# Second attention of a two-block transformer kernel: transposes two units and value products three units behind the scores, three probability buffers, newest unit first on VectorE

## The chip, the cores and the metric

One core of a Trainium2 chip runs the whole program. The metric is the device time of one execution in microseconds. Its engines work side by side, each through its own list of instructions in order, and wait for each other through semaphores: TensorE (PE, with PEld for its weight loads), VectorE (DVE), ScalarE (ACT), GpSimd (POOL) and SyncE (SP), which issues the transfers of the weights.

## What is computed

A first transformer block on 256 tokens is followed by a second block of two layers on 256 latent and 256 context tokens, all in float32. The change lies in the second block's attention, which has eight heads of two 64-wide halves each:

```
s = einsum('bqhcd,bkhcd->bchqk', q, k) * 64 ** -0.5      # c: the two halves of a head
p = softmax(s, axis=-1)
a = p[:, 0] - lam * p[:, 1]
o = einsum('bhqk,bkhe->bqhe', a, v)                       # e: 128 wide
```

Latent queries attend to all 512 keys. In the first of the two layers the context queries attend to the 256 context keys as well.

## The kernel before

The attention stage runs once in layer 0 and once in layer 1 and has a barrier ahead of it and behind it. It is cut into **units**, one for a head and a block of 128 queries (`units2`, L682). Layer 0 has 32 units: numbers 0 to 15 with 512 keys (long units), 16 to 31 with 256 keys (short units). Layer 1 has the 16 long units only.

A unit u goes through seven steps:

1. `scores2` (L977, PE, matmuls L984): two products, one for each half, into a pair of PSUM banks. The pair alternates by unit (`scores_bank`, L678), so scores of u wait until the exponentials of u-2 have been read.
2. `rows2` (L1916, DVE, L1923): the row maxima of both halves, negated, in one reduction.
3. `exps2` (L1408, ACT, L1416): two exponentials with the row sum as a by-product, into the probability buffer `AT_P`. There are two such buffers, so exponentials of u wait for the transposes of u-2.
4. `probs2` (L1926, DVE, L1931 to L1935): reciprocal of both sums, times minus lambda for the second, one scaling (L1934), one scale-and-add (L1935). The instructions follow each other through a semaphore.
5. `turn2` (L988, PE, L996): two or four transposes of 128x128 into PSUM tile `PA[u % 2]`. They also wait until the output of u-2 has been read from the same tile.
6. `turned2` (L1937, DVE, L1944): one copy of the transposed probabilities to `AT_T[u % 2]`.
7. `values2` (L1000, PE, L1005) multiplies by the values into `PA[u % 2]`, and `out2` (L1420, ACT, L1423) copies the result out.

The order on each engine is written out by hand in three loops. Iteration u of PE (L1009) holds scores of u, the first half of the filling work, transposes of u-1, the second half of the filling work, and value products of u-2. Iteration u of ACT (L1426) holds the exponentials of u, its share of the filling work, and the output copy of u-2. Iteration u of DVE (L1947) is:

```
probs2(u - 1)
rows2(u)
turned2(u - 1)
beside(...)
```

**Filling work** (`attention_fill`, L82; `beside`, L810, L1285, L1686) is matrix work on streamed weights that needs the same stage as cover. Two kinds exist. Each of units 0 to 23 of layer 0 takes a modulation chunk ("ada"): 1 MB of weights, PE matmuls at L827 in PSUM pair 0, and two DVE adds of half a row (L1705). Each of units 4, 12, 20 and 28 of layer 0, and 2, 6, 10 and 14 of layer 1, takes a gate chunk ("ga"): PE matmuls at L833 and one copy each on DVE (L1914) and ACT (L1406). A chunk's matmuls wait until PSUM pair 0 has been emptied of the last one. SP refills a ring of four 1 MB slots whenever a chunk is done (L734).

After the stage's closing barrier PE computes the time-step projection (L1129), 64 matmuls, for which the next DVE work waits (L1963), while POOL and ACT start on the attention's normalisation.

Of the kernel before, what the change touches and what calls it, by code (L numbers as in the profile page):

```python
# [8 lines left out]
P = 128  # L9
# [3 lines left out]
TT = 512  # L13
# [13 lines left out]
ACT = mybir.ActivationFunctionType  # L27
# [54 lines left out]
def attention_fill(la):  # L82


    if la == -1:
        return [([("gates", GATE_AT.index(u))] if u in GATE_AT else [])
                + ([("ada0", u)] if u < ADA_CHUNKS else []) for u in range(A_UNITS)]
    units = 32 if la == 0 else 16
    every = units // 4
    return [([(f"ga{la}", u // every)] if u % every == every // 2 else [])  # L90
            + ([(f"ada{la + 1}", u)] if la == 0 and u < ADA_CHUNKS else []) for u in range(units)]
# [95 lines left out]
L_Q, L_K, L_V, L_TMP = 0, 4096, 8192, 16384  # L187
# [4 lines left out]
def program(nc, xT, stream, params, rows, consts, rel_bias, rev_hot, w_dt, scratch, cs_rows, out):  # L192
    ctx = ExitStack()
    with ctx:  # L194
# [5 lines left out]
        def sem(name):  # L200
            if name not in made:
                made[name] = ctx.enter_context(nc.semaphore(name))
            return made[name]
# [18 lines left out]
        def area(at, *shape):  # L222
            n = int(np.prod(shape))
            assert at + n <= ARENA, (at, n)
            v = work[:, at:at + n]
            names = "abcd"[:len(shape)]
            if len(shape) == 1:
                return v
            return v.rearrange(f"p ({' '.join(names)}) -> p {' '.join(names)}",
                               **{k: s for k, s in zip(names, shape)})  # L230
# [9 lines left out]
        def c_(name, i=0, n=None):  # L240
            at, m = CONSTS[name]
            return con[:, at + i:at + i + (m if n is None else n)]

        ident = c_("ident")
# [354 lines left out]
        LQ, LK, LV = area(L_Q, KT, TT), area(L_K, KT, TT), area(L_V, 4, D)  # L599
        MRG = area(L_MRG, KT, TT)  # L600
        GA = area(ARENA - 4096, KT, TT)
        AT_P = [area(L_TMP + 1024 * i, 2, TT) for i in range(2)]
        AT_T = [area(L_TMP + 2048 + 512 * i, 4, P) for i in range(2)]
        ADA = [RSTD[:, CHUNK * i:CHUNK * (i + 1)] for i in range(2)]
        ROT_T = [area(L_TMP + 4096 + 256 * i, T1) for i in range(2)]
# [72 lines left out]
        def scores_bank(u):  # L678
            return PS if u % 2 == 0 else PB[:, 1]


        def units2(la):  # L682
            lat = [(h, qt, 0, TT) for h in range(8) for qt in range(2)]
            own = [(h, 2 + qt, T1, T1) for h in range(8) for qt in range(2)]
            return lat + (own if la == 0 else [])
# [61 lines left out]
        def _(pe):  # L747
# [170 lines left out]
            for la in range(DEPTH_2):  # L918
# [23 lines left out]
                for j in range(4):  # L942
# [3 lines left out]
                    for t in range(4):  # L946
# [6 lines left out]
                        i = 4 * j + t  # L953
# [21 lines left out]
                us = units2(la)  # L975

                def scores2(u):  # L977
                    h, qt, k0, nk = us[u]
                    if u >= 2:
                        pe.wait_ge(sem("w_exp"), LAYER["w_exp"] * la + 2 * (u - 1))  # L980
                    S = scores_bank(u)
                    for cc in range(2):
                        rows_ = slice(HD * cc, HD * cc + HD)
                        mm = pe.matmul(S[:, cc, 0:nk], LQ[rows_, h, qt * P:(qt + 1) * P],  # L984
                                       LK[rows_, h, k0:k0 + nk], start=True, stop=True)
                    mm.then_inc(sem("w_scores"), 1)

                def turn2(u):  # L988
                    h, qt, k0, nk = us[u]
                    n = nk // P  # L990
                    pe.wait_ge(sem("w_probs"), LAYER["w_probs"] * la + u + 1)

                    if u >= 2:
                        pe.wait_ge(sem("w_out_read"), LAYER["w_out_read"] * la + u - 1)
                    for i in range(n):
                        mm = pe.transpose(PA[u % 2][:, i * P:(i + 1) * P],  # L996
                                          AT_P[u % 2][:, 0, i * P:(i + 1) * P], ident)
                    mm.then_inc(sem("w_turns"), 1)

                def values2(u):  # L1000
                    h, qt, k0, nk = us[u]
                    n = nk // P
                    pe.wait_ge(sem("w_turned"), LAYER["w_turned"] * la + u + 1)
                    for i in range(n):
                        mm = pe.matmul(PA[u % 2][:, 0:P], LV[:, k0 // P + i, h * P:(h + 1) * P],  # L1005
                                       AT_T[u % 2][:, i, :], start=(i == 0), stop=(i == n - 1))
                    mm.then_inc(sem("w_out"), 1)

                for u in range(len(us) + 2):  # L1009
                    if u < len(us):  # L1010
                        scores2(u)
                        beside(attention_fill(la)[u], T, 0)
                    if 1 <= u <= len(us):
                        turn2(u - 1)
                    if u < len(us):
                        beside(attention_fill(la)[u], T, 1)
                    if u >= 2:
                        values2(u - 2)
                held.finish(ada_second)
                bar()  # L1020
                def project_z(g, tiles):
# [212 lines left out]
        def _(act):  # L1234
# [3 lines left out]
            copy = nc.scalar.activation  # L1238
# [138 lines left out]
            for la in range(DEPTH_2):  # L1377
# [25 lines left out]
                us = units2(la)  # L1403
# [4 lines left out]
                def exps2(u):  # L1408
                    h, qt, k0, nk = us[u]
                    b = u % 2  # L1410

                    act.wait_ge(sem("w_max"), LAYER["w_max"] * la + u + 1)
                    if u >= 2:
                        act.wait_ge(sem("w_turns"), LAYER["w_turns"] * la + u - 1)
                    for cc in range(2):
                        copy(AT_P[b][:, cc, 0:nk], scores_bank(u)[:, cc, 0:nk], ACT.Exp,  # L1416
                             bias=STAT[:, 2 * b + cc:2 * b + cc + 1],
                             accum_out=STAT[:, 4 + 2 * b + cc:5 + 2 * b + cc]).then_inc(sem("w_exp"), 1)

                def out2(u):  # L1420
                    h, qt, k0, nk = us[u]
                    act.wait_ge(sem("w_out"), LAYER["w_out"] * la + u + 1)
                    copy(LQ[:, h, qt * P:(qt + 1) * P], PA[u % 2][:, 0:P], ACT.Copy)\  # L1423
                        .then_inc(sem("w_out_read"), 1)

                for u in range(len(us) + 2):  # L1426
                    held.finish(ada_second)
                    if u < len(us):
                        exps2(u)
                        beside(attention_fill(la)[u], ga_out)  # L1430
                    if u >= 2:
                        out2(u - 2)
                held.finish(ada_second)
                bar()

# [177 lines left out]
        def _(v):  # L1613
# [6 lines left out]
            def then(ins):  # L1620

                steps[0] += 1
                ins.then_inc(sem("dve_step"), 1)
                v.wait_ge(sem("dve_step"), steps[0])
# [230 lines left out]
            for la in range(DEPTH_2):  # L1855
# [55 lines left out]
                us = units2(la)  # L1911
# [14 lines left out]
                def probs2(u):  # L1926
                    h, qt, k0, nk = us[u]
                    b = u % 2
                    v.wait_ge(sem("w_exp"), LAYER["w_exp"] * la + 2 * u + 2)
                    r0, r1 = STAT[:, 8 + 2 * b:9 + 2 * b], STAT[:, 9 + 2 * b:10 + 2 * b]  # L1930
                    then(vec.reciprocal(STAT[:, 8 + 2 * b:10 + 2 * b], STAT[:, 4 + 2 * b:6 + 2 * b]))  # L1931
                    then(vec.tensor_tensor(r1, r1, NEG_LAM[:, la:la + 1], ALU.mult))
                    p0, p1 = AT_P[b][:, 0, 0:nk], AT_P[b][:, 1, 0:nk]
                    then(vec.tensor_scalar(p1, p1, r1, None, ALU.mult))  # L1934
                    vec.scalar_tensor_tensor(p0, p0, r0, p1, ALU.mult, ALU.add).then_inc(sem("w_probs"), 1)  # L1935

                def turned2(u):  # L1937
                    h, qt, k0, nk = us[u]
                    b = u % 2
                    n = nk // P  # L1940
                    v.wait_ge(sem("w_turns"), LAYER["w_turns"] * la + u + 1)
                    if u >= 2:
                        v.wait_ge(sem("w_out"), LAYER["w_out"] * la + u - 1)
                    vec.tensor_copy(AT_T[b][:, 0:n, :], PA[b][:, 0:nk].rearrange("p (a b) -> p a b", a=n))\  # L1944
                        .then_inc(sem("w_turned"), 1)

                for u in range(len(us) + 1):  # L1947
                    if u >= 1:
                        probs2(u - 1)
                    if u < len(us):  # L1950
                        rows2(u)
                    if u >= 1:
                        turned2(u - 1)
                    if u < len(us):
                        beside(attention_fill(la)[u], ga_out)
                bar()
# [514 lines left out]
```

## Time and profile before

| what | value |
|---|---|
| median of 3 executions | 3326.34 us (3325.12 to 3330.06) |
| profiled execution, its own time | 3327.07 us |
| span of the profiled execution | 3325.3 us |
| PE busy | 3120.7 us, 94% of the span |
| DVE busy | 1227.8 us, 37% |
| ACT busy | 689.4 us, 21% |
| POOL busy | 538.3 us, 16% |
| mean granted TensorE clock | 0.972 of full |
| attention stage of layer 0 | 963.3 to 1142.2 us |
| attention stage of layer 1 | 2473.7 to 2566.9 us |

The two stages take 272 us together, 8% of the span. The span is the time between the first and the last instruction; 1.8 us of the profiled execution lie around it. PEclk in a row is the clock that was granted to TensorE as a share of 2.4 GHz: 1.00 is 2.4 GHz and 0.50 is 1.2 GHz. In a timeline row, the number in square brackets is the time for which the engine had been idle, and behind the arrow stands whose instruction ended the idle time.

### The profile page before, as it was taken

What the parts mean: (1) busy time and instruction counts of PE and PEld (TensorE: products, weight loads), DVE (VectorE), ACT (ScalarE), POOL (GpSimd) and SP (SyncE); (2) the same over time, 40 slices, a digit from 0 to 9 for tenths busy, and PEclk for the clock granted to TensorE, in tenths of its full rate; (3) what the DMA queues carried; (4) which work ended last, traced back from release to release, by engine and by line L of the source; (5) the groups of instructions that cost most, each with busy time, mean ns of one, the idle gap of its engine ahead of it and who ended that gap; (6) DMA issues with size and microseconds to landing.
All of it is one profiled execution on the core that took longest, in us unless ns stands there. A gap on an engine that the chain in (4) does not pass through costs nothing. (4 is left out here: it accounts for less than half of the span.)

```text
span 3325.3 us, 36073 instructions
## 1 busy us (share of the span) xinstructions
PE 3120.7 (94%) x14066; PEld 2394.6 (72%) x14066; DVE 1227.8 (37%) x2407; ACT 689.4 (21%) x1549; POOL 538.3 (16%) x550
## 2 busy tenths in 40 slices
PE   8998799997999899999999999998998999989998
PEld 6765688885864546666758678887876666678887
DVE  1243222204136454656523343342235555541101
ACT  1112011101013314444430020010113244440100
POOL 0000100001210002121213324442210122210100
PEclk9999899998999899999989999999999999989999
DMA  6464234341226222222212212222211322224332
GB/s 228 159 228 165 101 123 153 134 153 67 78 102 228 76 90 102 89 98 93 76 51 89 76 64 89 89 89 76 89 64 51 109 101 102 102 89 146 139 141 99
DMA packets 60827, 365.62 MB, mean 110 GB/s; under 512 B 5818, under 2 KB 17146, under 8 KB 18320
## 3 DMA queue, kind: packets, MB, share of 16 engines
q1 hardware_dynamic: 48768, 334.65, 27.9%
q10 hardware_dynamic: 10944, 25.36, 2.1%
q0 software_dynamic: 976, 3.67, 0.3%
q8 instruction: 97, 1.59, 0.2%
q14 instruction: 42, 0.34, 0.0%
HBM read 362.38 MB, written 1.28 MB: 109 GB/s over the span
## 5 line engine op out<-in xcount | busy, mean ns | idle before, releaser
L348 PE MATMUL PB<-H,ring 128*128 128x256 f32 (+1 forms) x2048 | 471.5, 394 | 26.9 <-ACT H L1387 20.7
L348 PEld LDWEIGHTS PB<-H,ring 128*128 128x128 f32 x2048 | 395.5, 194 | 102.9 <-issue 45.0
L1050 PE MATMUL PB<-H,ring 128*128 128x512 f32 (+1 forms) x1024 | 430.1, 567 | 0.0
L1050 PEld LDWEIGHTS PB<-H,ring 128*128 128x128 f32 x1024 | 192.9, 191 | 181.8 <-issue 175.6
L388 PE MATMUL PB<-work,ring 128*128 128x256 f32 x1280 | 279.7, 382 | 8.2 <-POOLq L284 7.2
L388 PEld LDWEIGHTS PB<-work,ring 128*128 128x128 f32 x1280 | 244.8, 191 | 43.0 <-issue 9.3
L1997 DVE SCALAR_TENSOR_TENSOR work<-PB,par,work 128x510 f32<-128x510 f32 (+3 forms) x256 | 182.1, 713 | 14.8 <-ACT work L1458 8.0
L1031 PE MATMUL PB<-ring,H 128*128 128x256 f32 x768 | 174.5, 382 | 4.9 <-DVE work L1997 4.9
L833 PE MATMUL PB<-H,ring 128*128 128x256 f32 (+1 forms) x640 | 177.6, 432 | 0.9 <-ACT mod L1282 0.9
L492 POOL TENSOR_TENSOR sums<-ring 128x512 f32<-128x512 f32 x53 | 68.4, 1290 | 670.9 <-PE PA L459 231.4
L348 PE MATMUL PB<-work,ring 128*128 128x256 f32 (+1 forms) x544 | 155.2, 447 | 7.7 <-POOLq L284 5.0
L1031 PEld LDWEIGHTS PB<-ring,H 128*128 128x128 f32 x768 | 143.1, 190 | 23.6 <-issue 5.7
L833 PEld LDWEIGHTS PB<-H,ring 128*128 128x128 f32 x640 | 121.1, 194 | 48.6 <-issue 35.0
L1502 ACT ACTIVATE work<-sums,work 128x128 f32<-128x128 f32 x384 | 119.0, 396 | 163.5 <-PE PA L1112 163.5
L459 PE MATMUL PB<-work,sums 128*128 128x256 f32 x680 | 150.8, 379 | 0.0
L348 PEld LDWEIGHTS PB<-work,ring 128*128 128x128 f32 x544 | 104.4, 193 | 56.9 <-issue 37.2
L459 PEld LDWEIGHTS PB<-work,sums 128*128 128x128 f32 x680 | 129.2, 190 | 17.6
L2297 POOL TENSOR_TENSOR work<-work 128x256 f32<-128x256 f32 x128 | 83.8, 679 | 289.3 <-PE PA L1112 289.3
L2281 POOL TENSOR_TENSOR work<-work 128x256 f32<-128x256 f32 x96 | 62.2, 667 | 381.8 <-ACT work L1482 312.7
L1112 PEld LDWEIGHTS PA<-work 128*128 128x128 f32 x768 | 102.2, 206 | 23.6 <-issue 11.5
L459 PE MATMUL PA<-work,sums 128*128 128x256 f32 x528 | 118.5, 379 | 0.0
L1841 DVE SCALAR_TENSOR_TENSOR work<-PB,par,work 128x254 f32<-128x254 f32 (+1 forms) x128 | 55.8, 477 | 169.0 <-ACT work L1361 164.8
(315 smaller groups left out, 4251.8 us busy)
## 6 DMA issues: line engine op xcount, KB each, us to landing
ring<-stream SPq DMA_DIRECT2D x315, 1024.0 KB, 4.8
sums<-cs_rows ACTq DMA_DIRECT2D x16, 1024.0 KB, 4.7
sums<-cs_rows ACTq DMA_DIRECT2D x16, 512.0 KB, 4.0
work<-scratch POOLq DMA_DIRECT2D x1, 2560.0 KB, 13.9
X<-xT SPq DMA_DIRECT2D x2, 1024.0 KB, 15.3
out<-H SPq DMA_DIRECT2D x1, 1024.0 KB, 4.8
con<-consts SPq DMA_DIRECT2D x1, 716.0 KB, 17.8
wdt<-w_dt POOLq DMA_DIRECT2D x1, 512.0 KB, 10.4
```

The costliest lines, as they stand in the source:

```text
L348: mm = pe.matmul(PB[:, pair, t, 0:T], ring[:, c % SLOTS, k, t * P:(t + 1) * P], rhs(k), start=(k == 0), stop=(k == KT - 1))
L388: mm = pe.matmul(PB[:, pair, t, 0:T], ring[:, c % SLOTS, k, t * P:(t + 1) * P], rhs(KT * part + k), start=(part == 0 and k == 0), stop=(pa ...
L459: mm = pe.matmul(fast_bank(side, bank)[:, col:col + T1], weight(k), right(4 * part + k), start=first and opens and k == 0, stop=last and k ...
L492: nc.gpsimd.tensor_tensor(su[:, 0], a21, a22, ALU.add).then_inc(sem("w_summed"), 1)
L833: mm = pe.matmul(PB[:, pair, t, 0:T], ring[:, c % SLOTS, k, t * P:(t + 1) * P], H[:, k, 0:T], start=(k == 0), stop=(k == KT - 1))
L1031: mm = pe.matmul(PB[:, pair, t // per, col:col + CHUNK], H[:, k, t * P:(t + 1) * P], ring[:, c % SLOTS, k, :], start=(k == 0), stop=(k == ...
L1050: mm = pe.matmul(PB[:, pair, t, 0:Tc], ring[:, c % SLOTS, k, t * P:(t + 1) * P], H[:, k, 0:Tc], start=(k == 0), stop=(k == KT - 1))
L1112: mm = pe.matmul(PA[t // 2][:, 256 * (t % 2) + HD * r:256 * (t % 2) + HD * r + HD], MB[r % 2][:, d, t, :], XC[r % 2][:, d, t, :], start=(d ...
L1502: ins = copy(MB[r % 2][:, d, t, :], BC[:, hp % 2, r % 2, d, t * P:(t + 1) * P], ACT.Relu, scale=-1.0, bias=CS[:, t, hh:hh + 1])
L1997: ins = vec.scalar_tensor_tensor(dst, src, par[:, W0 + 32 * tap + ch:W0 + 32 * tap + ch + 1], dst, ALU.mult, ALU.add)
L2281: gp.tensor_tensor(XD[d].rearrange("p (a b) -> p a b", a=4), XG[:, t, :].rearrange("p (a b) -> p a b", a=4), WD[:, t, heads].unsqueeze(2). ...
L2297: gp.tensor_tensor(XC[r % 2][:, d, :, :], XG[:, :, HD * r:HD * r + HD], DT[:, :, hh:hh + 1].broadcast_to([P, 4, HD]), ALU.mult)\
```

## The change

A third probability buffer is added in free memory. On PE the transposes move from one unit behind the scores to two, and the value products from two to three. On ACT the output copy moves from two units behind to three, and exponentials of u wait for the transposes of u-3 in place of u-2. On DVE an iteration takes the row maxima of the newest unit first, then the probabilities of the unit before, then the copy of the transposes of the unit before that. No instruction other than waits is added to or taken from a unit, and each loop gains one iteration at its end. The filling work keeps its unit numbers.

```diff
-        AT_P = [area(L_TMP + 1024 * i, 2, TT) for i in range(2)]
+        AT_P = [area(L_TMP + at_, 2, TT) for at_ in (0, 1024, 4608)]
...
-                for u in range(len(us) + 2):
+                for u in range(len(us) + 3):
                     if u < len(us):
                         scores2(u)
                         beside(attention_fill(la)[u], T, 0)
-                    if 1 <= u <= len(us):
-                        turn2(u - 1)
+                    if 2 <= u <= len(us) + 1:
+                        turn2(u - 2)
                     if u < len(us):
                         beside(attention_fill(la)[u], T, 1)
-                    if u >= 2:
-                        values2(u - 2)
+                    if u >= 3:
+                        values2(u - 3)
...
-                    if u >= 2:
-                        act.wait_ge(sem("w_turns"), LAYER["w_turns"] * la + u - 1)
+                    if u >= 3:
+                        act.wait_ge(sem("w_turns"), LAYER["w_turns"] * la + u - 2)
...
-                for u in range(len(us) + 2):
+                for u in range(len(us) + 3):
                     held.finish(ada_second)
                     if u < len(us):
                         exps2(u)
                         beside(attention_fill(la)[u], ga_out)
-                    if u >= 2:
-                        out2(u - 2)
+                    if u >= 3:
+                        out2(u - 3)
...
-                for u in range(len(us) + 1):
-                    if u >= 1:
-                        probs2(u - 1)
+                for u in range(len(us) + 2):
                     if u < len(us):
                         rows2(u)
-                    if u >= 1:
-                        turned2(u - 1)
+                    if 1 <= u <= len(us):
+                        probs2(u - 1)
+                    if u >= 2:
+                        turned2(u - 2)
                     if u < len(us):
                         beside(attention_fill(la)[u], ga_out)
```

Where a step reads or writes `AT_P`, the index `u % 2` becomes `u % 3`; all other buffers keep two copies.

## Rows read from the trace of the kernel before

**Rows 1.** Busy time by engine in stretches: both attention stages, one short unit.

```profile
core 0: us, PE busy (x) PEld busy (x) DVE busy (x) ACT busy (x) POOL busy (x), PEclk, DMA share, GB/s
963.30:1142.20 178.90, 153.70 (x937) 80.21 (x937) 100.62 (x243) 51.77 (x169) 0.00 (x0) 0.97 0.48 170
2473.70:2566.90 93.20, 73.89 (x384) 53.73 (x384) 54.97 (x101) 29.40 (x85) 0.00 (x0) 0.95 0.16 56
1097.50:1100.70 3.20, 2.71 (x26) 1.44 (x26) 2.49 (x9) 1.30 (x5) 0.00 (x0) 1.00 1.00 364
```

**Rows 2.** Waits in layer 1's attention stage: who waits for whom, total, times, longest.

```profile
PE PA L996 <- DVE work L1935: 18.3, 8, 5.1
...
DVE small L1931 <- ACT work L1416: 12.8, 12, 2.9
```

**Rows 3.** Timeline, one plain unit of layer 1: start, duration, engine, line.

```profile
2499.40 1.22 DVE L1923 TENSOR_REDUCE small<-PS 128x2 f32<-128x1024 f32 x1
...
2499.54 0.66 PE L996 MATMUL PA<-con,work 128*128 128x128 f32 x4 [1.76 <-DVE work L1935]
...
2500.53 0.68 DVE L1944 COPY work<-PA 128x512 f32<-128x512 f32 x1
...
2501.02 1.13 PE L984 MATMUL PB<-work 64*128 64x512 f32 x4
...
2502.13 0.17 DVE L1931 RECIPROCAL small<-small 128x2 f32<-128x2 f32 x1 [0.92 <-ACT work L1416]
...
2503.71 1.22 DVE L1923 TENSOR_REDUCE small<-PB 128x2 f32<-128x1024 f32 x1
```

**Rows 4.** Timeline, one long unit of layer 0 with a modulation chunk.

```profile
1010.05 1.22 DVE L1923 TENSOR_REDUCE small<-PB 128x2 f32<-128x1024 f32 x1
...
1010.19 0.66 PE L996 MATMUL PA<-con,work 128*128 128x128 f32 x4 [0.51 <-DVE work L1935]
...
1012.79 0.17 DVE L1931 RECIPROCAL small<-small 128x2 f32<-128x2 f32 x1 [0.38 <-ACT work L1416]
...
1012.87 1.13 PE L984 MATMUL PS<-work 64*128 64x512 f32 x4
...
1014.37 1.22 DVE L1923 TENSOR_REDUCE small<-PS 128x2 f32<-128x1024 f32 x1
```

**Rows 5.** Timeline, short units of layer 0: with a chunk, then without.

```profile
1099.13 0.49 DVE L1705 TENSOR_TENSOR rstd<-PB,rstd 128x128 f32<-128x128 f32 x2 [0.61 <-PE PB L827]
...
1100.85 0.44 PE L996 MATMUL PA<-con,work 128*128 128x128 f32 x2 [0.51 <-DVE work L1935]
...
1108.59 0.17 DVE L1931 RECIPROCAL small<-small 128x2 f32<-128x2 f32 x1 [0.73 <-ACT work L1416]
```

**Rows 6.** Timeline, a unit of layer 1 with a gate chunk beside it.

```profile
2548.79 1.13 PE L984 MATMUL PS<-work 64*128 64x512 f32 x4
...
2551.48 1.22 DVE L1923 TENSOR_REDUCE small<-PS 128x2 f32<-128x1024 f32 x1
...
2558.28 1.13 PE L984 MATMUL PB<-work 64*128 64x512 f32 x4
...
2559.46 1.23 DVE L1923 TENSOR_REDUCE small<-PB 128x2 f32<-128x1024 f32 x1
```

**Rows 7.** Timeline, the first units of layer 0 and of layer 1.

```profile
968.75 0.17 DVE L1931 RECIPROCAL small<-small 128x2 f32<-128x2 f32 x1 [2.46 <-ACT work L1416]
...
974.65 1.22 DVE L1923 TENSOR_REDUCE small<-PS 128x2 f32<-128x1024 f32 x1
...
2479.11 0.17 DVE L1931 RECIPROCAL small<-small 128x2 f32<-128x2 f32 x1 [2.85 <-ACT work L1416]
...
2485.01 1.22 DVE L1923 TENSOR_REDUCE small<-PS 128x2 f32<-128x1024 f32 x1
```

**Rows 8.** Timeline, the last row of layer 1's attention stage.

```profile
2566.55 0.28 ACT L1423 ACTIVATE work<-PA 128x128 f32<-128x128 f32 x1 [0.77 <-PE PA L1005]
```

**Rows 9.** Stretches behind each attention stage (columns as in rows 1).

```profile
1142.20:1155.00 12.80, 12.80 (x60) 12.80 (x61) 0.00 (x0) 6.18 (x3) 2.04 (x2) 0.50 0.00 0
2566.90:2574.30 7.40, 7.38 (x65) 7.39 (x66) 0.00 (x0) 4.48 (x3) 1.18 (x2) 1.00 0.00 0
```

More of the change, by code:

```diff
@@ L996, in turn2 @@
                         mm = pe.transpose(PA[u % 2][:, i * P:(i + 1) * P],
-                                          AT_P[u % 2][:, 0, i * P:(i + 1) * P], ident)
+                                          AT_P[u % 3][:, 0, i * P:(i + 1) * P], ident)
                     mm.then_inc(sem("w_turns"), 1)
@@ L1412, in exps2 @@
                     act.wait_ge(sem("w_max"), LAYER["w_max"] * la + u + 1)
-                    if u >= 2:
-                        act.wait_ge(sem("w_turns"), LAYER["w_turns"] * la + u - 1)
+                    if u >= 3:
+                        act.wait_ge(sem("w_turns"), LAYER["w_turns"] * la + u - 2)
                     for cc in range(2):
-                        copy(AT_P[b][:, cc, 0:nk], scores_bank(u)[:, cc, 0:nk], ACT.Exp,
+                        copy(AT_P[u % 3][:, cc, 0:nk], scores_bank(u)[:, cc, 0:nk], ACT.Exp,
                              bias=STAT[:, 2 * b + cc:2 * b + cc + 1],
@@ L1932, in probs2 @@
                     then(vec.tensor_tensor(r1, r1, NEG_LAM[:, la:la + 1], ALU.mult))
-                    p0, p1 = AT_P[b][:, 0, 0:nk], AT_P[b][:, 1, 0:nk]
+                    p0, p1 = AT_P[u % 3][:, 0, 0:nk], AT_P[u % 3][:, 1, 0:nk]
                     then(vec.tensor_scalar(p1, p1, r1, None, ALU.mult))
```

## Prediction, made before the changed kernel was run

> **What bounds the kernel now.** I first read the share of busy time: PE is busy for 94% of the span, so time is lost mostly where PE waits. Then I cut out the two attention stages. In layer 1's stage of 93.2 us PE is busy for 73.9 us and DVE for 55.0, and in layer 0's stage of 178.9 us for 153.7 and 100.6 [rows 1]: neither is full, so something is waiting in a circle. The waits name it: PE waits for DVE's last probability step, and DVE's reciprocal waits for ACT's exponentials [rows 2].
>
> One plain unit of layer 1 shows the circle. DVE starts the row maxima at 2499.40, its reciprocal can only start at 2502.13, when the maxima and both exponentials have run (2.73 us), and the next maxima start 1.58 us later, behind the four probability steps [rows 3]. Maxima, exponentials, probabilities, next maxima: 2.73 + 1.58 = 4.31 us a unit, because DVE's order puts the probabilities of a unit ahead of the maxima of the next. In that circle DVE is idle for 0.92 us, and PE, whose work is 2.61 us (transposes at 2499.54, end of scores at 2502.15), for some 1.7 [rows 3]. A long unit with a modulation chunk has the same circle, 4.32 us, with DVE idle for 0.38 and PE for 0.51 [rows 4]. Short units have DVE idle for 0.61 and PE for 0.51 with a chunk, and DVE for 0.73 without [rows 5]. Beside a gate chunk PE has no gap: scores to scores is 9.49 us, and DVE and ACT wait [rows 6].
>
> **What the change does to a plain unit.** With maxima of u, then probabilities of u-1, then the copy of u-2, ACT's exponentials of u run while DVE works on older units, so the circle is cut. Let R(u) be the start of the maxima of u. What bounds a unit is then DVE's own work, 4.31 - 0.92 = 3.39 us [rows 3]. The new waits must fit in it. PE's scores of u+1 stand behind the value products of u-3, which need DVE's copy of u-3, the last act before R(u). Transposes to scores takes 1.48 us in PE's order and scores 1.13 [rows 3], so even from R(u) the scores of u+1 are done by R(u) + 2.6, before 3.39. The exponentials now wait for transposes three units back, a buffer more, and cost nothing. No DMA or SP instruction moves; only the time at which a chunk is released does.
>
> Layer 1 has 13 intervals from unit 2 on, four with a gate chunk and nine plain: 9 x 0.92 = **8.3 us**.
>
> **Gate chunks.** PE is the bound there, so its 9.49 us stay. Before, scores started 2.69 us ahead of the maxima (2548.79, 2551.48), and behind the chunk 1.18 ahead (2558.28, 2559.46), which gives 7.98 us between maxima [rows 6]. Afterwards scores start about 1 us behind R(u-1), behind the value products, so 2.35 ahead of R(u), and the interval is 9.49 + 1.18 - 2.35 = 8.32. That is 0.34 us more, four times: **-1.4 us**. In layer 0 the same sum has a smaller difference of the leads, since PE is nearly as full as DVE; I take nothing for its four, with 0.3 us each either way in the range.
>
> **Long units with a chunk**, twelve intervals of layer 0. DVE's work is 4.32 - 0.38 = 3.94 us and PE's 4.32 - 0.51 = 3.81 [rows 4]. DVE bounds, by little: 12 x 0.38 = **4.6 us**. Two waits come close. PE's chunk of u needs PSUM pair 0, which DVE frees at the end of its iteration u-1, at R(u). Then chunk and value products take 2.68 - 0.66 = 2.0 us, scores 1.13 [rows 4], so scores of u+1 are done by R(u) + 3.2, in time. The transposes of u-1 stand next on PE and wait for the output copy of u-3, which ACT now does behind the exponentials of u: R(u) + 2.73 + 0.28 = 3.0 [rows 3, 8]. Slack is 0.2 us. Behind this wait stand the next chunk, the value products and the scores for which DVE's next maxima wait, so it is the place to look at.
>
> **Short units.** Seven intervals with a chunk: DVE would give 0.61 and PE 0.51, so PE becomes the bound and I take 7 x 0.51 = **3.6 us**. A chunk of 1 MB (1.05 MB in decimal) each 2.71 us asks for 387 GB/s where the trace has 364 at a DMA share of 1.00 [rows 1]; at 364 the chunk takes 2.88 us and 1.2 us of the gain go. The ring holds four chunks and the gate chunk's long unit refills it, so I take the full value and keep 1.2 for the range. Six without a chunk: 6 x 0.73 = **4.4 us**. DVE is their bound, since PE has no chunk product in them.
>
> **First units.** Today the maxima of unit 2 stand behind the probabilities of unit 1. Afterwards the maxima of 1 run while DVE waits for the first exponentials, so the maxima of 2 start behind the probabilities of 0: 2479.11 + 1.58 = 2480.69 in place of 2485.01 in layer 1, **4.3 us**; in layer 0 968.75 + 1.58 + 0.4 for the chunk's adds = 970.7 in place of 974.65, **3.9 us** [rows 7]. A bound below is 2 us each, if PE finds scores of 2 late.
>
> **Last units.** From the last maxima to the stage's last copy is 7.4 us today (2559.46 to 2566.83) [rows 6, 8]. Afterwards DVE does maxima 1.13, probabilities 1.58, copy 0.68, probabilities 1.58, two copies 1.36, then value products 0.9 with their start (1.48 - 0.66 and a little) and the output 0.3 [rows 3, 8]: 7.5, and with the delays between engines 7.8 to 8.1. I take **-0.6 us** for each layer, -1.2.
>
> **The sum.** Layer 1: 8.3 - 1.4 + 4.3 - 0.6 = 10.6. Layer 0: 4.6 + 3.6 + 4.4 + 3.9 - 0.6 = 15.9. Together 26.5 us from the profiled execution's own 3327.07 (span 3325.3 and 1.8 around it), so 3300.6; this execution lies 0.7 us above the median of 3326.34, so against the median I forecast 3299.9, rounded 3300. Behind both stages stands a barrier, and the work behind it needs nothing but the stage, so what is saved there stays saved.
>
> **A rule that bears on the size.** Two DVE instructions without a wait follow each other closer than their durations: maxima of 1.22 us and the copy behind them start 1.13 apart [rows 3]. The copy and the next maxima would then also close up by 0.1 us, which over 21 DVE-bound long units gives 2 us more than my sum. The Trainium skill, VectorE: DVE Perf Modes, section "The DRAIN you can't avoid", says that the gap behind an instruction is the same with and without semaphores; by it there is nothing more to gain. I leave the 2 us out and let the range hold them.
>
> **The rivals.**
>
> *The clock stays up behind layer 0.* Behind layer 0's stage PE runs at a granted clock of 0.50, 60 matmuls in 12.8 us, where behind layer 1's it has 1.00 and 65 in 7.4 [rows 9]. Before the drop PE was only half full, in short plain units. These lose 0.73 us each [rows 5] and keep the same matmuls. If the clock then holds at 2.4 GHz, the 64 matmuls take 6.4 us less: 3293.5, with some 2 us more from what follows. Against it: the tail with its thin PE work remains. The Trainium skill, TensorE: Matmul & The Clock Gate, Part 1, says that the array is throttled by default and recent activity releases it; by that rule a fuller stage makes this the outcome. That the same stage in layer 1 ended at 1.00 agrees, but the low clock also came in between fuller units. Chance 0.22.
>
> *ACT's output copy becomes PE's wait.* The slack of 0.2 us above is used up by the delay of semaphores, and units with a chunk stay at their old length. The gain loses 4.6 + 3.6: 3308. The chunk units' DVE idle time would then be at the maxima and name PE's scores. Chance 0.11.
>
> *Slower: the clock drops in the long chunk units of layer 0.* At a half clock a matmul behind the stage takes 0.213 us in place of 0.114 [rows 9], 1.9 times. PE's 3.81 us would be 7.1, and it would bound the unit at 7.1 for 3.94. The twelve long units alone would lose 12 x 3.2 = 38 us: 3338. From nine such units on it is slower than today. Against it: PE's idle time in these units falls from 0.51 to 0.13 us, and they run at 1.00 in the trace today. Chance 0.03.
>
> *Little changes.* A wait I have not seen restores the old circle in most units, so that only the first units gain, 8 us less 1.2: 3319.5. The bound for "same" is this. Chance 0.04.
>
> **How the numbers follow.** The forecast case keeps 0.60. Its own ends: below, 2 us closing up, 1.2 for layer 0's gate units, 2 for low-clock moments of today that go, so 3295; above, 1.2 for DMA, 1.2 for gate units, 3 for first units that start late, so 3305. The range reaches to the fast clock's case with part of its extra and to the ACT case: 3290 to 3309, leaving out the last two and the ends, less than 2 in 10. A measurement of this kernel tells some 0.2% (6.7 us) from no change. Faster by over that are the forecast, the first two rivals and part of the rest: 0.93. Within: 0.04. Slower: 0.03.
>
> **What the profile after would show.** Right: plain units of layer 1 every 3.3 to 3.4 us with DVE without gaps and the idle time before the reciprocal gone; long chunk units at 3.9; short ones 0.5 and 0.7 us shorter than today; maxima of unit 2 about 4 us earlier in each stage; layer 0's stage 16 us shorter and layer 1's 11. Wrong: DVE idle before the maxima, released by PE's scores, or PE idle before the transposes, released by ACT's output copy. A granted clock of 1.00 behind layer 0's stage would be the first rival. The whole forecast would be wrong if the stages shrank but the stretch behind them grew.

## The result and the profile after

| what | before | after |
|---|---|---|
| median of four executions each | 3327.21 us | 3288.72 us (3287.92 to 3290.90) |
| profiled execution, its own time | 3327.07 us | 3288.54 us |
| span | 3325.3 us | 3286.7 us |
| mean granted TensorE clock | 0.972 | 0.978 |

The ratio is 0.9885 with a 95% interval of 0.9868 to 0.9902: faster by 1.15%, 38.5 us in both the medians and the profiled executions. I had forecast 3300 with a range down to 3290. The direction was right, the size was not: the time lies 1.3 us below the range.

Below, a plain unit has no filling work beside it, a chunk unit has a modulation chunk and a gate unit a gate chunk. The length of a unit is the time from the start of its row maxima to the start of the next unit's.

First the busy time of both stages, which answers to rows 1.

```profile
core 0: us, PE busy (x) PEld busy (x) DVE busy (x) ACT busy (x) POOL busy (x), PEclk, DMA share, GB/s
961.50:1122.30 160.80, 149.89 (x936) 78.71 (x936) 97.74 (x243) 50.77 (x169) 0.00 (x0) 1.00 0.52 190
2448.00:2528.60 80.60, 71.15 (x385) 52.21 (x385) 53.99 (x101) 29.18 (x85) 0.00 (x0) 0.98 0.17 64
```

PE does the same work in 18 and 13 us less. From the starts of the maxima in both traces, the whole difference can be laid out by place:

| place | before | after | saved |
|---|---|---|---|
| start to first maxima of layer 0 | 964.67 | 962.89 | 1.8 |
| layer 0, maxima of unit 0 to unit 31 | 171.60 | 154.18 | 17.4 |
| from there to the time-step projection | 5.93 | 5.49 | 0.4 |
| projection of layer 0 to first maxima of layer 1 | 1332.83 | 1326.81 | 6.0 |
| layer 1, maxima of unit 0 to unit 15 | 84.43 | 71.13 | 13.3 |
| from there to the projection | 7.46 | 8.09 | -0.6 |
| all behind | 758.38 | 758.11 | 0.3 |

A plain unit of layer 1 (rows 3 answer to it):

```profile
2486.48 0.63 PE L996 MATMUL PA<-con,work 128*128 128x128 f32 x4 [0.52 <-ACT work L1423]
2486.78 1.21 DVE L1923 TENSOR_REDUCE small<-PS 128x2 f32<-128x1024 f32 x1
...
2487.91 0.15 DVE L1931 RECIPROCAL small<-small 128x2 f32<-128x2 f32 x1
...
2488.01 1.13 PE L984 MATMUL PB<-work 64*128 64x512 f32 x4
...
2489.49 0.68 DVE L1944 COPY work<-PA 128x512 f32<-128x512 f32 x1
...
2490.09 1.22 DVE L1923 TENSOR_REDUCE small<-PB 128x2 f32<-128x1024 f32 x1
```

Maxima come every 3.31 us in place of 4.31 and the reciprocal follows the maxima with no idle time: the circle of rows 3 is gone, and DVE's own work is the bound. The copy starts 0.60 us ahead of the next maxima though it takes 0.68. I had counted it to its end, because rows 3 have an idle time behind it. Scores start 2.08 us ahead of their maxima (2488.01 to 2490.09), a lead that matters at the gate units. PE's transposes wait for ACT's output copy, by 0.52 us here, and nothing waits for them in turn.

A long unit with a chunk (rows 4 answer to it):

```profile
1002.61 1.23 DVE L1923 TENSOR_REDUCE small<-PB 128x2 f32<-128x1024 f32 x1
...
1003.08 1.07 PE L827 MATMUL PB<-ring,cact 128*32 128x256 f32 x16
...
1005.17 1.13 PE L984 MATMUL PS<-work 64*128 64x512 f32 x4
...
1005.94 0.48 DVE L1705 TENSOR_TENSOR rstd<-PB,rstd 128x128 f32<-128x128 f32 x2
...
1006.35 1.23 DVE L1923 TENSOR_REDUCE small<-PS 128x2 f32<-128x1024 f32 x1
```

It takes 3.74 us, and now neither DVE nor PE has idle time of note; the copy on ACT further down tells which of the two is the bound. The waits in layer 1's stage (columns as in rows 2) say the same in total:

```profile
DVE small L1923 <- PE PB L984: 5.3, 4, 1.5
PE PA L996 <- ACT work L1423: 5.1, 7, 1.6
...
DVE small L1931 <- ACT work L1416: 1.7, 1, 1.7
```

DVE waits 1.7 us for exponentials in place of 12.8, all of it in the first unit. What is left ahead of the maxima is mostly DVE's wait for scores, 5.3 us in four times.

Last the end of layer 0's stage and the stretch behind it (columns as above), which rows 9 answer to:

```profile
1112.85:1117.07 4.22, 3.00 (x21) 1.99 (x22) 4.01 (x12) 2.37 (x10) 0.00 (x0) 1.00 0.65 248
1117.07:1122.50 5.43, 3.43 (x22) 2.60 (x22) 3.92 (x13) 2.02 (x8) 0.00 (x0) 1.00 0.01 3
1122.60:1135.40 12.80, 12.80 (x78) 9.69 (x79) 4.66 (x8) 10.48 (x9) 3.25 (x4) 1.00 0.00 0
```

The clock is 1.00 to the end of the stage and behind it: 12.8 us hold 78 matmuls where rows 9 have 60 at 0.50. The 64 matmuls of the time-step projection take 7.36 us in place of 13.92, and 6.0 of these 6.6 us reach the table's fourth row. It is the first rival, to which I gave 0.22.

### The profile page after: what moved, and what is told of

Same layout as the page of the kernel before. It is cut to its first block and busy times, and to the rows that moved or that the text cites. A ratio compares the mean times of both kernels' runs of the same rounds, so it can differ in the third digit from the quotient of the medians.

```text
span 3286.7 us, 36071 instructions
## 1 busy us (share of the span) xinstructions
PE 3104.2 (94%) x14066; PEld 2383.2 (73%) x14066; DVE 1224.8 (37%) x2407; ACT 688.5 (21%) x1549; POOL 538.1 (16%) x550
## 6 DMA issues: line engine op xcount, KB each, us to landing
work<-scratch POOLq DMA_DIRECT2D x1, 2560.0 KB, 13.9
```

## The experiments

Each kernel is compared with the kernel before, whose medians beside these runs were 3325.6 to 3326.0 us.

**The parts of the change alone.** First DVE's order alone, on the kernel before:

```diff
                 for u in range(len(us) + 1):
+                    if u < len(us):
+                        rows2(u)
                     if u >= 1:
                         probs2(u - 1)
-                    if u < len(us):
-                        rows2(u)
                     if u >= 1:
                         turned2(u - 1)
```

> The kernel before with only DVE's order changed (maxima of u, probabilities of u-1, copy of u-1); PE and ACT as before, two probability buffers. Theory A (the skew on PE is what lets the new order pay): PE's scores of u+1 now stand behind the transposes of u-1, which wait for probabilities that follow the maxima of u, so a new circle closes: maxima 1.13 + probabilities 1.6 + transposes and value products 1.5 + scores 1.2 = some 5.5 us a plain unit of layer 1 in place of 4.31, more with a chunk; the time rises by 30 to 60 us, to 3360 to 3385. Theory B (DVE's order alone breaks the circle, the skew adds little): plain units at 3.4 to 4.1 us, time 3295 to 3320.

Measured: 3431.76 us, ratio 1.0317 (1.0300 to 1.0334). Slower by 3%, and by more than either theory said. In the timeline of a plain unit of layer 1 the circle of theory A stands complete:

```profile
2575.53 1.12 PE L996 MATMUL PA<-con,work 128*128 128x128 f32 x4 [2.90 <-DVE work L1935]
...
2576.44 1.92 PE L1005 MATMUL PA<-work 128*128 128x128 f32 x8
...
2578.28 1.16 PE L984 MATMUL PB<-work 64*128 64x512 f32 x4
...
2579.50 1.22 DVE L1923 TENSOR_REDUCE small<-PB 128x2 f32<-128x1024 f32 x1 [2.12 <-PE PB L984]
...
2582.35 0.90 PE L996 MATMUL PA<-con,work 128*128 128x128 f32 x3 [2.90 <-DVE work L1935]
```

Transposes wait for the probabilities (2.90 us idle), scores stand behind them and the value products, and the maxima wait for scores (2.12 us idle). Maxima to transposes is 2.85 us. At full clock the rest would take some 2.7, as foreseen, but with PE thin the clock fell to 0.84 over 2570 to 2600 and it takes 3.97: 6.8 us a unit. Theory A stands, with its size missed by the clock and by the units with a chunk, 6.7 us and more in place of 4.32. DVE's new order needs the skew on PE.

Then the skew and the third buffer with DVE's old priority:

```diff
                 for u in range(len(us) + 2):
+                    if 1 <= u <= len(us):
+                        probs2(u - 1)
                     if u < len(us):
                         rows2(u)
-                    if 1 <= u <= len(us):
-                        probs2(u - 1)
```

> The changed kernel with DVE's old priority: probabilities of u-1 ahead of the maxima of u; skew on PE and ACT and three buffers kept. Theory A (the circle maxima, exponentials, probabilities, next maxima is DVE's order alone): plain units of layer 1 stay at 4.31 us and the time is that of before, 3325 to 3331, a little above for the longer end of each stage. Theory B (the depth behind the scores gives part of the gain): plain units below 4.1 us, time below 3318.

Measured: 3307.86 us, ratio 0.9942 (0.9925 to 0.9958). Neither theory has it. A gate chunk's unit and the plain unit behind it, in layer 1:

```profile
2510.19 1.13 PE L984 MATMUL PS<-work 64*128 64x512 f32 x4
...
2514.36 1.22 DVE L1923 TENSOR_REDUCE small<-PS 128x2 f32<-128x1024 f32 x1
...
2519.68 1.13 PE L984 MATMUL PB<-work 64*128 64x512 f32 x4
...
2520.86 1.23 DVE L1923 TENSOR_REDUCE small<-PB 128x2 f32<-128x1024 f32 x1
...
2523.60 0.17 DVE L1931 RECIPROCAL small<-small 128x2 f32<-128x2 f32 x1 [0.92 <-ACT work L1416]
...
2525.18 1.22 DVE L1923 TENSOR_REDUCE small<-PS 128x2 f32<-128x1024 f32 x1
```

The plain unit is 4.32 us long with 0.92 us idle ahead of the reciprocal, as theory A says. But the gate unit takes 6.50 in place of 7.98, and in layer 0 the first takes 16.59 in place of 18.14. PE, freed from waiting for the newest probabilities, runs further ahead of DVE and spends that lead in the gate unit. The leads give the lengths: scores start 4.17 us ahead of the gate unit's maxima here and 1.18 behind the chunk, and 9.49 + 1.18 - 4.17 = 6.50. With the 2.70 of before the same sum gives 7.97, with the 2.08 of the changed kernel 8.59. So the skew alone gives half of the gain, most of it from units in which PE is the bound, and I had looked for it only in DVE's. Of the 18.9 us between the two traces, gate units make 14.0 (3.6 of them in the two units of layer 1 that had been at a low clock), short chunk units, 2.96 us now, 2.0, and the way from layer 0's projection to layer 1 4.4; 1.5 us are lost elsewhere.

The clock behind layer 0 was 1.00 here too, though the short plain units are 2.96 us long as before:

```profile
1130.00:1137.10 7.10, 4.80 (x23) 4.08 (x21) 3.53 (x10) 2.02 (x8) 0.00 (x0) 0.56 0.01 2
1137.10:1150.00 12.90, 12.90 (x78) 9.79 (x79) 4.72 (x8) 10.57 (x9) 3.34 (x4) 1.00 0.00 0
```

It fell within the stage's end and was back at 1.00 ahead of the projection. What brought it back, no run here shows.

The third buffer taken away from the changed kernel:

```diff
-        AT_P = [area(L_TMP + at_, 2, TT) for at_ in (0, 1024, 4608)]
+        AT_P = [area(L_TMP + at_, 2, TT) for at_ in (0, 1024)]
...
-                    if u >= 3:
-                        act.wait_ge(sem("w_turns"), LAYER["w_turns"] * la + u - 2)
+                    if u >= 2:
+                        act.wait_ge(sem("w_turns"), LAYER["w_turns"] * la + u - 1)
```

> The changed kernel with two probability buffers in place of three, so the exponentials of u wait for the transposes of u-2, which PE now does behind the scores of u. Theory A (the transposes of u-2 are done by the end of the maxima of u, the third buffer is not what pays): 3288 to 3291. Theory B (the third buffer is needed): the exponentials wait behind the chunk products in each unit with a chunk, DVE's reciprocal or the copy waits, 3298 to 3320.

Measured: 3291.91 us (3288.70 to 3293.32). Its median is 0.9 above theory A's range, but the stages are those of the changed kernel to 0.02 us (154.17 and 71.11 between first and last maxima); what differs is 2.3 us ahead of the first maxima. The third buffer buys nothing.

**The clock behind layer 0.** On the kernel before, extra matmuls fill PE's idle time:

```diff
+                def spare(n):
+                    for i in range(n):
+                        pe.matmul(PB[:, 0, 0, 0:T1], ident, H[:, 0, 0:T1], start=True, stop=True)
...
+                    if la == 0 and u == 29:
+                        pair_, before_ = GROUPS["ga0"][3]
+                        pe.wait_ge(evacuated[pair_], 2 * before_ + 2)
+                    if la == 0 and u >= 29:
+                        spare(3 if u < 33 else 1)
                     if 1 <= u <= len(us):
                         turn2(u - 1)
```

> The kernel before with 13 extra matmuls of 256 columns into a free PSUM bank in the idle times of PE in units 29 to 31 of layer 0 and the stage's end (results unused). Theory A (the 6 us saved behind layer 0's stage come from the granted clock, which thin PE work ahead of it had lowered): the stretch behind the stage runs at 1.00 as in the changed kernel and the time falls to 3319 to 3323 with nothing else changed. Theory B (the 6 us have another cause, such as transfers or the other engines' timing): the stretch stays at 0.50 or stays as long, 3326 to 3330.

Measured: 3320.31 us over ten executions (3315.67 to 3323.23), ratio 0.9979 (0.9970 to 0.9989). The stretch behind the stage, columns as above:

```profile
1130.00:1132.50 2.50, 2.50 (x16) 2.05 (x16) 2.11 (x6) 0.73 (x4) 0.00 (x0) 1.00 0.27 111
1139.30:1152.00 12.70, 12.68 (x77) 9.72 (x78) 4.50 (x8) 10.35 (x9) 3.11 (x4) 1.00 0.00 0
```

Here, too, it runs at 1.00, with 77 matmuls in 12.7 us, and 1327.2 us lie between the stages in place of 1332.8. The units of layer 0 kept their lengths. In layer 1, where the instructions are those of before, the stretch of maxima is 1.9 us shorter (82.55 for 84.43) and the end behind it 1.3 longer: the moments of low clock lie elsewhere in it, and the second gate unit is 7.97 us long in place of 9.49. Between the stages, work that nobody needs, done where PE idled, gives 5.6 us: theory A.

The counter-test slows three units of the changed kernel on DVE:

```diff
+                def slow():
+                    then(vec.tensor_tensor(RSTD[:, :], X[:, 0, :], X[:, 1, :], ALU.add))
...
                     if u < len(us):
                         rows2(u)
+                    if la == 0 and u >= 29:
+                        slow()
```

> The changed kernel with one extra 512-wide DVE add (result unused) behind the maxima of units 29 to 31 of layer 0, which makes these units about as long as before. Theory A (how thin PE's work is at the end of layer 0's stage decides the granted clock behind it): the clock falls in or behind these units in some executions, profile or times show 3 us more for the adds and up to 6 more for the clock, 3291 to 3298. Theory B (the clock no longer falls whatever the tail's length, because the stage before it is fuller): 3290 to 3292, stretch behind the stage at 1.00.

Measured: 3297.54 us (3295.92 to 3299.21), 8.8 above the changed kernel.

```profile
1113.80:1118.00 4.20, 1.81 (x12) 1.02 (x10) 3.93 (x11) 2.38 (x10) 0.00 (x0) 0.91 0.00 0
1118.00:1123.80 5.80, 4.17 (x16) 3.37 (x16) 3.94 (x10) 0.83 (x3) 0.00 (x0) 0.50 0.01 3
1123.80:1136.60 12.80, 12.79 (x60) 12.79 (x61) 0.00 (x0) 6.18 (x3) 2.04 (x2) 0.50 0.00 0
```

The clock is at 0.50 again, with 60 matmuls in 12.8 us exactly as in rows 9, and 1333.0 us lie between the stages. The last two intervals of the stage are 0.7 us longer each, and the stage's end 2.4. From both sides, what PE does in the last units and in the stage's end decides over 6 us behind a barrier.

**Short chunk units.** Seven were to save 0.51 us each; they saved 2.7 together. The intervals behind units 16 to 18 stayed at 3.1 to 3.2 us. I had seen a danger there in the transfers:

```diff
-                    sp.dma_start(ring[:, j, :, :],
+                    sp.dma_start(ring[:, j, 0:KT // 2, :],
...
```

> The changed kernel loads only the first half of every weight chunk from the fifth on, so half the weight traffic is left out and the second half of each product uses old weights. Theory A (in short chunk units 16 to 20 of layer 0 PE is the bound because it still carries long units' transposes and value products): the intervals between their maxima stay at 3.1 to 3.2 us and layer 0's stage stays within 0.3 us of 154.2. Theory B (weight transfers bound them, as the 364 GB/s suggested): the intervals fall to 2.7 and the stage gets 1 to 2 us shorter. The whole time may fall elsewhere, where other stages wait for weights.

Measured: 3292.97 us, and the stage 154.16; the intervals are 3.17, 3.21, 3.09 with half of every chunk left out (a DMA share of 0.43) as with all of it. Theory A. In the changed kernel this stretch shows PE without a gap at a DMA share of 0.88:

```profile
1053.00:1061.00 8.00, 8.00 (x83) 5.09 (x74) 7.37 (x22) 3.50 (x15) 0.00 (x0) 1.00 0.88 330
```

The first short units carry the transposes and value products of long ones, up to three units back. The skew that makes the gain moves this work behind the border of the two kinds. From unit 19 on the intervals are 2.65, as forecast.

**What bounds the units now.** The copy of the transposes goes from DVE's loop (second part) to ACT's (first part):

```diff
                     if u >= 3:
                         out2(u - 3)
+                    if 2 <= u <= len(us) + 1:
+                        turned2(u - 2)
...
-                    if u >= 2:
-                        turned2(u - 2)
```

> The changed kernel with the copy of the transposes moved from DVE to ACT, behind the output copy of u-3. Theory A (in the changed kernel DVE's own work bounds plain units and ACT has room): plain units of layer 1 fall from 3.31 to 2.8 us, bounded by the way from the exponentials over the output copy, transposes, value products and scores; short plain units from 2.11 to 1.8, long chunk units stay at 3.73 since PE is full; 3281 to 3286. Theory B (PE or ACT's waits already bound plain units): intervals within 0.1 us of those of the changed kernel, 3288 to 3292.

Measured: 3290.03 us (3288.30 to 3292.65), no gain. The units did what theory A says, and the time did not follow:

```profile
2487.58 1.22 DVE L1935 TENSOR_REDUCE small<-PS 128x2 f32<-128x1024 f32 x1
...
2490.54 1.22 DVE L1935 TENSOR_REDUCE small<-PB 128x2 f32<-128x1024 f32 x1 [0.17 <-PE PB L984]
...
2493.26 1.22 DVE L1935 TENSOR_REDUCE small<-PS 128x2 f32<-128x1024 f32 x1
```

Plain units alternate between 2.96 and 2.72 us, but the gate units grew to 9.48 from 8.59 (the first to 10.41 from 9.90), because scores now lead their maxima by 1.18 us only. A group of four takes 17.9 us in place of 18.5, while PE's own work in it is 9.49 + 3 x 2.62 = 17.35 [rows 3, 6]: PE is nearly full, and a faster DVE only takes away the lead that PE had at the gate chunk.

```profile
2492.00:2505.00 13.00, 13.00 (x70) 9.70 (x68) 6.45 (x14) 5.51 (x16) 0.00 (x0) 1.00 0.21 81
```

The stages shrank by 2.7 and 0.9 us, and 2.4 came back at their ends and behind. DVE bounds the plain units of the changed kernel, and PE is close behind. The long chunk units stayed at 3.74 us and the short ones at 2.64 with less work on DVE: there PE is the bound.

Whether ACT's output copy holds PE back:

```diff
+                    late = u < len(us) and any(name.startswith("ga") for name, j in attention_fill(la)[u])
+                    if u >= 3 and not late:
+                        out2(u - 3)
                     if u < len(us):
                         exps2(u)
                         beside(attention_fill(la)[u], ga_out)
-                    if u >= 3:
+                    if u >= 3 and late:
                         out2(u - 3)
```

> The changed kernel with ACT's output copy of u-3 ahead of the exponentials of u, except in units with a gate chunk. Theory A (PE's transposes wait for this copy, which sets how far ahead PE runs, but DVE's own work bounds the units): PE's idle time behind ACT's output copy goes, plain units stay at 3.31 us, gate units of layer 1 fall by 0.1 to 0.3 us from 8.59; the time is the control's to 1 us below. Theory B (that wait is what bounds plain units): plain units fall below 3.2 us and the time is 3 us or more below the control.

Measured: 3289.60 us against a control of 3291.94. Plain units stay at 3.31, and the gate units at 8.59, so not even the small gain of theory A came. The waits in layer 1 show why:

```profile
ACT work L1423 <- PE PA L1005: 24.3, 16, 2.3
...
PE PA L996 <- DVE work L1938: 4.4, 8, 1.4
```

PE's transposes now wait for DVE's last probability step instead (L1938 is L1935 of the kernel before), 4.4 us in all against 5.1 for the output copy. The wait was real and never on the path: my second rival is dead from both sides.

**The first gate unit of layer 1.** It takes 9.90 us and the others 8.59. Six extra matmuls fill PE's wait ahead of it:

```diff
                 for u in range(len(us) + 3):
+                    if la == 1 and u == 2:
+                        for i in range(6):
+                            pe.matmul(PB[:, 0, 0, 0:T1], ident, H[:, 0, 0:T1], start=True, stop=True)
```

> The changed kernel with six extra matmuls of 256 columns where PE waits for the first exponentials of layer 1. Theory A (the low granted clock after that wait costs 1.3 us in the first gate-chunk unit and some tenths before it): first gate unit 8.6 us in place of 9.90, time 1.3 to 2 us below the control. Theory B: same length as the control or longer by the extra matmuls.

> The changed kernel once more, as the control of the two beside it. Theory A: the two stages and the stretch behind the first are the same to 0.1 us, and what differs between executions lies ahead of the first stage; 3287 to 3291. Theory B: the granted clock behind layer 0's stage also falls in some profiles of this kernel, then 3293 to 3297.

> copy_on_act with six extra matmuls of 256 columns into a free bank where PE waits for the first exponentials of layer 1 (results unused). Theory A (the 9.90 us of the first gate-chunk unit of layer 1, against 8.59 of the others, is the granted clock that this wait had lowered): the first gate unit falls to the length of the others and the time is 1 to 2.5 us below copy_on_act. Theory B (another cause): the first gate unit stays 1.3 us longer than the others and the time is the same as copy_on_act or 0.5 us above.

Measured: 3289.46 us with the extra matmuls and 3291.94 for the control; on top of the copy on ACT 3287.95 against 3290.03. The changed kernel, then the one with extra matmuls:

```profile
2450.50:2453.00 2.50, 0.00 (x0) 0.00 (x0) 1.23 (x2) 2.31 (x4) 0.00 (x0) 1.00 0.06 23
2455.50:2458.00 2.50, 2.50 (x7) 1.99 (x6) 2.22 (x5) 1.45 (x4) 0.00 (x0) 0.50 0.00 0
```

```profile
2454.00:2456.50 2.50, 1.93 (x9) 0.74 (x7) 1.06 (x4) 2.50 (x8) 0.00 (x0) 1.00 0.00 0
2456.50:2459.00 2.50, 2.50 (x12) 2.22 (x13) 2.39 (x6) 0.97 (x5) 0.00 (x0) 1.00 0.00 0
```

Behind 2.5 us without a matmul, themselves still at 1.00, the clock of the first is 0.50; the second stays at 1.00. The first gate unit is 8.21 us and layer 1's stretch of maxima 1.7 us shorter (71.12 to 69.45), and 2.8 with the copy on ACT (70.27 to 67.51). In the first pair 0.6 us of it came back in the rest of the program, in the second nothing. Theory A, though the unit fell further than the 8.6 foreseen. The control's stages repeat to 0.05 us. The medians of the executions can't place these versions against the changed kernel: the changed kernel itself gave 3288.72 in one comparison and 3291.94 in the other, and the best, 3287.95, has executions from 3282 to 3289. I claim 1.7 us of stage for the extra matmuls, and no proven winner.

## Why the prediction was wrong

**Right:** the circle and how it is cut. Rows 3 and 4 gave 3.39 and 3.94 us a unit, and 3.31 and 3.74 came. The first units saved 4.3 and 3.9 us, both to the tenth. The last units of layer 1 cost 0.6, as forecast.

**Wrong: the choice between the forecast and the first rival,** the step that failed, 6.0 of the 12 us by which the forecast saving of 26.5 fell short. I priced the clock behind layer 0 at 6.4 us and gave it 0.22, arguing that "the tail with its thin PE work remains". So the sum had nothing for it. The tail did remain, PE busy for 3.43 of 5.4 us, and the clock still held. The two experiments from both sides show that PE's work at the stage's end moves it. The length of the short units alone does not decide: with the skew only they were as long as before, and the projection ran at 1.00. The Trainium skill, TensorE: Matmul & The Clock Gate, Part 1, says that recent activity releases the throttle. The changed kernel and the extra matmuls agree with it, at 1.00, and so does the slowed end in reverse, at 0.50. But in the kernel before and behind the slowed end the clock stayed at 0.50 through 12.8 us in which PE was busy throughout. By that rule alone it should have risen there; the traces decide, and why it did not is open.

Had I taken the rival, its 3293.5 would still have been 4.8 us too high, through the sizes below and what lies ahead of the stages.

**Wrong in size:**

| term | forecast | measured |
|---|---|---|
| plain units, layer 1 | 8.3 | 9.1 |
| gate units, layer 1 | -1.4 | -0.16 |
| long chunk units | 4.6 | 7.1 |
| short chunk units | 3.6 | 2.7 |
| short plain units | 4.4 | 5.1 |
| gate units, layer 0 | 0 | -1.3 |
| last units of layer 0 | -0.6 | +0.4 |

- Plain and long units: DVE's work was taken to the end of a copy (0.68) where the next start counts (0.60), and once more behind the chunk's adds. I had the 2 us that this is worth and set them aside with a citation of the Trainium skill, VectorE: DVE Perf Modes, "The DRAIN you can't avoid". That section also says that a next instruction that is not held starts earlier, which I did not use. The traces decide: 0.60 from start to start without a wait. I also had DVE as the bound of the long units, by little, at 3.94 us; with less work on DVE they stayed at 3.74, so it is PE. The long units saved 0.59 each, more than even PE's idle time of 0.51 in rows 4, where scores were taken at 1.13 to their end; the transposes follow them 1.06 behind when nothing is waited for.
- Gate units of layer 1: the sum of leads gave 0.34 us more each, and the plain comparison is 8.59 against 7.98, so 0.6: the lead is 2.08, where I took 2.35. But two of the four of before were 2.1 and 1.5 us longer than that (10.07 and 9.49), and only one of after is (9.90); these moments at low clock, of which only the one of the changed kernel was put to a test, stood as "2 us" in my range and not in the sum.
- Gate units of layer 0: the same loss of lead that I took for nothing cost 1.3.
- Short chunk units: the border between long and short ones was left out; transfers, which I feared, have no part.

**Outside the change:** 1.8 us lie ahead of the first stage. Over twelve profiles with the same code up to there, the first maxima come at 960.3 to 967.8 us. The forecast could not know that. How much of it is in the medians is not shown: the changed kernel measured once more gave 3291.94, inside the range. So it is partly chance that the time fell below the range; the failed step does not hang on that, since the clock behind layer 0 was 1.00 in both traces of the changed kernel.

The remaining rivals: no clock fell in the long units, no old circle came back, and no output copy bound PE.

## What to carry to other kernels

When PE, DVE and ACT pass a unit around in a circle, changing the order on one engine alone can close a worse circle: ask for each engine what stands behind the instruction that will now wait. Here the order alone cost 106 us, the skew alone gave 18, and the order on top of the skew another 19; the two gains lie mostly in different units, because a lead that PE gains is spent where PE is the bound. Count the work between two starts rather than durations, and treat a thin end of a stage ahead of a barrier as a possible clock drop that is paid behind it: if a row ahead of the change shows 0.50, a change to PE's work there has to be priced both with it and with it gone, and neither case is the safe one.

## What was not expected of the hardware

- One DVE add of 0.7 us in each of the last three units of a stage moves the granted clock from 1.00 to 0.50, where it stays through a full stretch of 64 small matmuls with PE busy all the time. These take 13.9 us in place of some 7.4; extra matmuls whose result nobody reads bring it back.
- The stages repeat to 0.05 us from profile to profile (154.16 to 154.19 us between first and last maxima of layer 0 in the changed kernel, its control, after_head, half_loads, out_first and two_buffers), while the time ahead of them scatters over 7 us. For a change of a stage the trace resolves far more than the median.
- With skew_only the clock fell to 0.50 within the stage's end and was back at 1.00 for the stretch behind it, so a fall alone does not set the price: 0.56 over the 7.1 us of the end, and 1.00 in the stretch.
